# A slot schedule on one core: attention steps spread by slot weight, first mix eight slots later

## The reference

```python
h = x @ w_in                          # q | k | v | u, 512 columns each
k_all = concat(k_hist, k); v_all = concat(v_hist, v)
a = _stick_breaking(q, k_all, v_all)  # 8 heads of 64, queries in blocks of 128
p = _pool_mix(u, ...)                 # trailing means over 2, 4, 8, 16 frames
mix = concat(a, p) @ w_out
x1 = layer_norm(ALPHA * x + mix)
y = layer_norm(ALPHA * x1 + (silu(x1 @ w_gate) * (x1 @ w_up)) @ w_down)
# in a block of queries, for one head:
z = q @ k.T / 8; log_beta = log_sigmoid(z)
log_1m = where(mask, log_beta - z, 0)
a = where(mask, exp(log_beta + reversed_cumsum(log_1m) - log_1m), 0) @ v
```

## Time and profile before

| | us |
|---|---|
| median of 3 runs | 2573.28 (2573.16 to 2575.05) |
| profiled execution, its own time | 2575.84 |
| its span | 2574.1 |
| PE busy in it | 2514.1 (98%) |
| DVE busy | 1573.4 (61%) |
| ACT busy | 1154.6 (45%) |
| POOL busy | 1178.1 (46%) |

### The profile page before, as it was taken

The page is one execution under the profiler, slowest core; times in us unless marked ns, Lnnn a source line. Parts: engine busy times, 40 slices in busy tenths (PEclk is TensorE's granted clock), DMA queues, the critical chain, the costliest instruction groups (busy, mean ns, idle before and its releaser), DMA issues.

```text
span 2574.1 us, 37571 instructions
## 1 busy us (share of the span) xinstructions
PE 2514.1 (98%) x13882; PEld 2144.2 (83%) x13882; DVE 1573.4 (61%) x2125; ACT 1154.6 (45%) x1932; POOL 1178.1 (46%) x1028
## 2 busy tenths in 40 slices
PE   9999999999999999999999999999999999999998
PEld 9978898787878878878788887878878887899997
DVE  3266347675444366787744567787775355866776
ACT  4365327664323145666532265656554213433333
POOL 4465537754323145565532174556653214354434
PEclk9999999999999999999999999999999999999999
DMA  6788956773456233444263244343533522223232
GB/s 212 221 260 273 348 194 192 224 218 115 131 158 213 82 107 115 124 122 119 82 229 128 91 115 119 103 112 110 155 91 115 202 66 91 98 91 115 92 97 85
DMA packets 210134, 374.30 MB, mean 145 GB/s; under 512 B 29760, under 2 KB 104128, under 8 KB 207904
## 3 DMA queue, kind: packets, MB, share of 16 engines
q1 hardware_dynamic: 209952, 371.89, 45.8%
HBM read 303.73 MB, written 68.09 MB: 144 GB/s over the span
## 4 chain that ended last, share of the span: by engine, by line
PE 84%; DVE 7%; DMA 2%; issue 2%; ACT 2%; POOL 1%; SPq 1%; DVEq 0%; ACTq 0%; POOLq 0%
PE bank L1315 26%; PE bank L1377 19%; PE bank L1265 11%; PE bank L1219 7%; PE bank L1323 7%; PE bank L1116 5%; PE bank L1164 4%; PE bank L1132 4%; DVE left L1947 1%; DMA gw_lo_raw<-in_w_in_dram 1%; DVE acc L1985 1%; PE bank L1242 1%; DMA v_st<-v_cache_scratch 1%; ACT bank L1502 0%; DVE stats L1967 0%
## 5 line engine op out<-in xcount | busy, mean ns | idle before, releaser
L1315 PE MATMUL bank<-x1T,gw_hi 128*128 128x512 f32 (+1 forms) x2336 | 712.1, 388 | 3.7 <-DVE hT_lo_raw L2061 2.3
L2547 POOL TENSOR_TENSOR beta<-beta,left 128x512 f32<-128x512 f32 (+2 forms) x326 | 352.6, 1082 | 350.6 <-DVE left L1947 349.9
L1315 PEld LDWEIGHTS bank<-x1T,gw_hi 128*128 128x128 f32 x2336 | 418.3, 188 | 83.6 <-issue 3.4
L1315 PE MATMUL bank<-x1T,gw_lo 128*128 128x512 f32 (+1 forms) x1168 | 447.7, 383 | 0.0
L2574 POOL TENSOR_TENSOR gw_lo<-gw_lo_raw,gw_hi 128x1024 fp32r<-128x1024 f32 x70 | 181.9, 2599 | 423.1 <-ACT gw_hi L1569 422.9
L1492 ACT ACTIVATE aT<-bank 128x512 fp32r<-128x512 f32 (+2 forms) x326 | 173.8, 533 | 428.4 <-PE bank L1132 379.8
L1265 PE MATMUL bank<-x1T,gw_hi 128*128 128x256 f32 (+2 forms) x1472 | 355.0, 334 | 2.0 <-DVE later_qk L2267 1.0
L2242 DVE TENSOR_TENSOR acc<-bank,acc 128x512 f32<-128x512 f32 x312 | 213.4, 686 | 210.9 <-PE bank L1377 207.4
L1932 DVE TENSOR_TENSOR aT<-bank,aT 128x512 fp32r<-128x512 f32 (+2 forms) x326 | 197.0, 604 | 201.0 <-ACT aT L1492 199.8
L1377 PE MATMUL bank<-dw_hi,hT_hi 128*128 128x512 f32 x728 | 295.1, 405 | 9.8 <-issue 5.8
L1377 PE MATMUL bank<-dw_lo,hT_hi 128*128 128x512 f32 x728 | 286.5, 394 | 0.0
(11 more groups left out here) (223 smaller groups left out, 4702.8 us busy)
## 6 DMA issues: line engine op xcount, KB each, us to landing
gw_lo_raw<-in_w_gate_dram SPq DMA_DIRECT2D x88, 512.0 KB, 3.7
gw_lo_raw<-in_w_up_dram SPq DMA_DIRECT2D x88, 512.0 KB, 3.8
dw_lo_raw<-in_w_down_dram SPq DMA_DIRECT2D x86, 512.0 KB, 4.4
gw_lo_raw<-in_w_in_dram SPq DMA_DIRECT2D x64, 512.0 KB, 4.6
k_st<-kT_scratch SPq DMA_DIRECT2D x160, 128.0 KB, 4.2
v_st<-v_scratch SPq DMA_DIRECT2D x80, 256.0 KB, 4.3
q_st<-qT_scratch SPq DMA_DIRECT2D x128, 128.0 KB, 3.9
wo_raw<-in_w_out_dram SPq DMA_DIRECT2D x16, 1024.0 KB, 5.6
```

The source lines that it names most:

```text
L1315: m = pe.matmul(gu_bank(g, n)[:, 0:w], gw[L % 4][a][:, k, :], x1T[x][:, k, first:first + w], start=k == 0 and s == 0, stop=k == KD - 1 and ...
L2547: pool.tensor_tensor(x[:, 0:w], x[:, 0:w], left[n % RL][:, 1:w + 1], ALU.mult).then_inc(a_done, 1)
```

## The change

Before, a tick's slot was proportional to its place in the list. Now a slot counts 2 where it is a projection slot (below 256) and 3 where it is a feed-forward slot. A range that lies in slots of one kind is dealt out as before, so only block 1's attention feels the weights. Its range now begins at slot 196, block 0's attention ends at 136, and the whole first mix, norm included, comes eight slots later.

```diff
     def spread(ticks, first, end):
         weights = [...]
+        passed_by = list(itertools.accumulate(2 if s < FP else 3 for s in range(first, end)))
         total, before = sum(weights), 0
         for tick, w in zip(ticks, weights):
-            due.setdefault(first + before * (end - first) // total, []).append(tick)
+            due.setdefault(first + sum(x * total <= before * passed_by[-1] for x in passed_by), []).append(tick)
             before += w
 
-    A_FROM = [72, 188, 456, 721]
-    M_FROM = [128, 372, 637, 956]
-    M_END = [188, 456, 721, 1022]
-    NORM_FROM, NORM_EVERY = [196, 460, 725, 1022], [8, 6, 6, 3]
+    A_FROM = [72, 196, 456, 721]
+    M_FROM = [136, 372, 637, 956]
+    M_END = [196, 456, 721, 1022]
+    NORM_FROM, NORM_EVERY = [204, 460, 725, 1022], [8, 6, 6, 3]
```

## The result

The changed kernel takes 2590.28 us in the median of six runs (2587.36 to 2592.73), the kernel before 2574.97 on the same chip (2573.16 to 2578.58): a ratio of 1.0054, 95% interval 1.0044 to 1.0065. It is slower by half a per cent, 15 us, and its time lies above the range that was given. The profiled execution took 2592.73 us with a span of 2591.0, 16.9 longer than that of the kernel before.

The account below looks back on a forecast made before the run. PE, busy 2514.1 of 2574.1 us, was taken as the bound, so only its idle and lower-clock time could move. Terms -1.8 -1.2 +0.5 -3.7 -1.2 +5.5 +1.3 +3.0 gave +2.4 on the median 2573.28: 2575.7 us, range 2565 to 2584.6.

Parts of the forecast that it names:

- Block 0's attention: 44 ticks over 64 slots for 56: fewer PE waits for the scan and for `later_d`; -1.8 us (-3.1 to 0).
- slot 215: Pool product in block 1's attention: slot 213 has no tick now, so the low part comes sooner; -1.2 us (-1.7 to 0).
- slots 225 and 237: Where the next two pools' low parts are made: each gets a tick it had not; +0.5 us (0 to 1.7).
- the two clusters: Waits and lower clock near 459 and 490 us, behind late weight loads: first -1.2 us, second -3.7 us.
- The first mix, slot 163: PE waits at the pool product for a low part behind `wo_lo` and a late weight load; +5.5 us (0.3 to 8.9).
- Rival (d): Slot 163's wait is its full 8.9 us with the lower clock after it; +7.6 us, 2580.9; chance 0.16.
- x's own loads beside the next block's: First mix, ticks 12 to 15: nothing due on PE before M0.18, five slots after the last as before; 0.
- The end of the first mix: Slots 187 to 194: `pair_lo` stands behind a norm tick, PE waits one centring; +1.3 us (0 to 3.7).
- Feed-forward slots: Slots 256 to 294 take 31 ticks for 18, drawing DVE nearer to PE; +3.0 us (0 to 7.8).
- rival (c): Slower in slots 256 to 294: DVE becomes the bound, PE loses 8 us instead of 3; 2580.7; chance 0.17.
- The blocks after: Blocks after the rescheduled stretch are dealt as before; 0.
- Rival (e): Port rule: `wo_lo` comes behind a whole low part of POOL's, 2.4 us more; +4.8 us, 2578.1; chance 0.05.

Follow-up runs that it names:

- e4: Changed kernel with block 0's attention dealt over slots 72 to 128, as before the change; ratio 1.0042 to the kernel before.
- e3: Changed kernel with wo_hi made at the end of slot 161 on ACT and wo_lo behind the rest of slot 161 on DVE; ratio 1.0042 to the kernel before.
- e5: Changed kernel with the first mix dealt four slots later still (143 to 200), its norm from 208; 2587.98 us, ratio 1.0038 to the kernel before.
- e9: Changed kernel with SP issuing cached-key loads and cached-value stores three slots later, behind the weight load; 2584.95 us, ratio 1.0031 to the kernel before.
- e14: e9 with block 2 storing only 64 of 512 columns of its key and value outputs; ratio 1.0017 to the kernel before.
- e13: Changed kernel with block 2 storing only 64 of 512 columns of its key and value outputs; ratio 1.0037 to the kernel before.
- e6: Changed kernel with the first pair's gate product put ahead of slot 263's attention tick on DVE; ratio 1.0034 to the kernel before.
- e1: Changed kernel with the new weights 2 and 3 but the old lists of slots; 2578.53 us, ratio 1.0007 to the kernel before.
- e7: Weights 2 and 3 with the old lists of slots, and the gate's product first in slot 263; 2572.95 us, ratio 0.9984 to the kernel before.

## Why the prediction was wrong

Its forecast was that new waits and gains nearly cancel. The gain in block 1's attention came about as worked out, the new waits came larger, and two kinds of loss had been put at nothing: the lower clock behind the new waits, and late weight loads in block 0. By its own steps:

- **Block 0's attention, -1.8 (-3.1 to 0).** A step that failed: up to +6.0, outside its bounds. What was counted came: the scores' waits for `left` fell from 1.9 to 1.1 us and those for `later_d` from 1.2 to none. Not counted was that the moved ticks could meet a late weight load, which they did at 209 us: 2.5 us of waiting for `beta`, 1.6 for `aT` just before, and a stretch at 1.2 GHz behind them (e4). Only in its last sentence does the prediction allow for such a load. The rest is the clock after the first wait for `k_st`, 3.8 us for 3.7 before: it was low for 7 us and not 3.5. That is not the change's: e3, e5 and e9 have the same slots there and 3.5 us, as e4 has.
- **Block 1's attention: slot 215, slots 225 and 237, the two clusters, -5.6 together.** About right: -4.2, with the second cluster gone and the first one standing (2.5 us of waiting and its 3.5 us of clock), as the prediction left two thirds of it.
- **The first mix, slot 163, +5.5 (0.3 to 8.9).** The step that failed here is the value, not the mechanism, which was right in each link. The value took two things off the upper bound of 8.9: 2.05 us for a load that lands in 6.15, and 1.4 for an SP that is less late. Neither came: the load took 8.3 us, and it went out 6.1 us after the turning of values that begins slot 156, later than the 5.4 of the kernel before (the prediction's 5.0). The waiting was 9.1 us, 2.2 of it already at slot 160 and 6.9 at slot 163; that the 6.9 equals the prediction's middle figure is chance. The second miss is the clock, which the forecast put at nothing here: 10.2 us at 1.2 GHz, 3.0 of them lost. With what was idle before taken off, the stage lost 11.3. Rival (d), with a chance of 0.16, was the right case, and its 3.4 + 1.75 came close: 3.6 and 3.0. With the prediction's other terms as they were it gives 2580.9 for 2590.28 measured; the rest is mostly block 0.
- **Why the load is late** was taken as given from the earlier trace rows. The runs show the memory (e14 against e9; in the changed kernel the DMA share is 1.05 from 300 to 325 us), SP's order only where the memory leaves room (nothing in e9, 1.8 us in e14 against e13), and `wo` behind the load, 3.1 us (e3). In the kernel before the load is 8.2 us under way too, but the sums of slots 157 to 160 cover it. The shift took the cover away. In e5, where no sums stand there either, PE still waits 3.7 us though no `wo_lo` is in front.
- **x's own loads beside the next block's, 0.** Right in the changed kernel, and wrong four slots later, where the same cover was counted on: 4.5 us in e5.
- **The end of the first mix, +1.3.** About right: +0.8. PE waits 1.1 us in front of slot 194's matmuls at 411.70; the profile names no releaser, but DVE's `later_qk`, behind a centring, ended at 411.60.
- **Feed-forward slots, +3.0.** Right in size, +2.6, and wrong in kind. It was not DVE drawn nearer to PE over 85 us, but one product of 0.6 us that stood behind a scan of 1.28, 2.7 us of waiting and 3.5 of clock; rival (c) is refuted (e6, and e1, where ticks are dense as well).
- **The blocks after, 0.** One more stretch at 1.2 GHz near 970 us, at most +1.75. It is absent in e1, e3, e4 and e7 and present in e5, e6 and e9, so it does not go with the slots; it was not looked into.
- **Rival (e), the port.** The `wo_lo` in question took 2.29 us, its price when alone. It was the other side that was late: POOL's next low part of the weights, beside the second `wo_lo`, took 4.10 us, for 2.35 the one before:

```profile
311.55 2.35 POOL L2618 TENSOR_TENSOR gw_lo<-gw_lo_raw,gw_hi 128x1024 fp32r<-128x1024 f32 x1 [3.33 <-ACT gw_hi L1682]
318.10 4.10 POOL L2618 TENSOR_TENSOR gw_lo<-gw_lo_raw,gw_hi 128x1024 fp32r<-128x1024 f32 x1 [4.20 <-ACT gw_hi L1682]
```

On this pair the trace agrees with the rule of the Trainium skill (SBUF — State Buffer, "SBUF: two separate sides") that one of the two waits for the other. No PE wait hung on it here.

The memory in the mix moved 403 GB/s from 300 to 325 us. The Trainium skill (HBM Reference, "Specifications (TRN2)") gives some 425 GB/s for one core that streams alone, bounded by its 16 DMA engines; the trace agrees with a stretch near that bound, 5% below it.

## What to carry to other kernels

When work is moved, ask not only what it will stand in front of but what it has been covering: here the late load was in the trace before, and the sums that moved away were its cover. A wait that grows past those already in the profile can take a longer stretch at the lower clock with it, so price the two together, and count of that stretch only the part in which PE works. When two profiles are compared at a wait, measure from one instruction of PE to another as well: here a wait fell from 6.9 to 4.1 us and nothing was won (e9). And where a schedule costs a few us, look for the single instruction that PE wants and that stands last in its slot: two such orders and one on SP (e3, e6, e9) won back all that the shift of slots lost, and one of them turned the neutral weights into a gain (e7).

## What was not expected of the hardware

- After waits of 2.2 and 6.9 us the granted clock was 1.2 GHz for 10.2 us, of which PE worked 6.0. Behind the wait for `k_st`, at 129 us, it was low for 7 us in the changed kernel and e6 (3.8 and 3.7 us of waiting), for 3.5 in the kernel before, e1 and e4 (3.7, 3.6 and 3.3) and not at all in e7 (3.2). So waits of one length were followed by different stretches.
- Under a DMA share of 1.04 to 1.05 a load of 512 KB took 12.0 us when it was issued earlier and 8.3 when issued later (e9 and the changed kernel): counted from the start of slot 156, an issue 3.7 us earlier bought nothing.
- Leaving out stores (0.9 of the 12.1 MB that moved between 264 and 302 us) brought the same load 2.6 us sooner where it was issued early (e14 against e9), and 0.8 us where it was issued late (e13).
